# Splitting every product of the first down projection over the two 64-row halves of the array

## The chip, the cores and the metric

The kernel runs on one NeuronCore of a Trainium2 chip. The time of a kernel is that of one execution on the device, in microseconds (us). TensorE (PE in the rows) multiplies, VectorE (DVE) and ScalarE (ACT) work on tiles and take results out of PSUM, SyncE (SP) and GpSimd (POOL) issue transfers.

## The reference

One layer of a decoder trunk, 256 tokens of width 2048, in float32. Three attention branches and a gated merge come first; the change touches only the last step, the MLP:

```python
h = rms_norm(x, norm_mlp_pre[l])
u = jnp.square(jax.nn.relu(h @ w_up[l]))          # (256, 2048) @ (2048, 8192)
x = x + rms_norm(u @ w_down[l], norm_mlp_post[l]) # (256, 8192) @ (8192, 2048)
```

## The kernel before

**Numbers.** Each float32 operand is held as two float32r parts, a high and a low one. A product of two operands is three matmuls: high by high, high by low, low by high. ScalarE makes the high part of a weight tile (`w_hi`, L975), VectorE the low part (`w_lo`, L1367).

**Units.** Weights come in units: 256 rows of a weight matrix (two blocks k of 128) by 512 columns, 512 KB, in a ring of four slots. TensorE uses a unit in `unit` (L504 to L521): for each of the two token halves t, for each of the two k, three matmuls of 128 rows by 512 columns, 12 in all. The stationary operand is a 128 by 128 piece of the activations, which is loaded anew for each matmul (PEld, LDWEIGHTS); the moving operand is 512 columns of the weights. The results of token half t are summed in one PSUM bank.

**Chunks.** A chunk is all units of one set of 512 output columns. The first down projection, `down0`, has the first 4096 rows of `w_down`: 4 chunks of 16 units, the first written out, the other three a loop. So it has 4 x 16 x 12 = 768 matmuls. They use banks 0 (t = 0) and 1 (t = 1) in every chunk. `down1` does the same with the other 4096 rows and adds the result to that of `down0`, which waits in `y` in SBUF. Between them stands `up1`, which makes the second half of `u`; its first chunk uses banks 0 and 1 again. Transposes of `u` go through banks 6 and 7; in `down0` there is one group of 8, after the second unit of the first chunk.

**Emptying the banks.** The last matmul of token half 0 of a chunk raises `half_done`, the last of the chunk (as of each unit) raises `unit_used`. In `down0` before, VectorE copies bank 0 to `y` after `half_done` (`copy_out`, L1384) and raises `evac_v`, and ScalarE copies bank 1 after `unit_used` (L1336) and raises `evac_s`. In `down1` VectorE does both, by adding bank 0 or 1 to `y` (L1971). TensorE waits for these counts before the first matmul into a bank in the next chunk (`free`). In VectorE's order, which is the order of the code, the work on bank 0 stands ahead of the split of a weight unit that belongs to the last unit of the chunk, and (in `down1`) the work on bank 1 behind it. The splits run three units ahead (`LEAD`).

Of the kernel before, what the change touches and what calls it, by code (L numbers as in the profile page):

```python
# [21 lines left out]
ACT = mybir.ActivationFunctionType  # L22
AX = mybir.AxisListType.X

P = 128
# [5 lines left out]
W = 512  # L31
UR = 2
RING = 4
# [21 lines left out]
U0, C0 = {}, {}  # L55
# [5 lines left out]
UNITS = _u  # L61
UNITS_BEFORE_BRANCH = U0["branch"]

V_OF = {"gate": 0, "branch": 6, "out": 2, "down1": 2}
S_OF = {"branch": 0, "out": 2, "down1": 2, "gate": 2, "up0": 2, "up1": 2}
T_OF = {"v_a": 0, "v_c": 0, "gate": 0, "out": 0, "down0": 0, "down1": 0}
V0, S0, T0 = {}, {}, {}
_v = _s = _t = 0
# [93 lines left out]
def wait(eng, sem, value):  # L162

    if not (isinstance(value, int) and value <= 0):
        eng.wait_ge(sem, value)


def trunk(nc, x, rel_bias, w_in, cmp_k_pos, cmp_v_pos, cmp_k_w1, cmp_k_w2, cmp_v_w1, cmp_v_w2, diff_lambda,
# [10 lines left out]
    def sem(name):  # L179
        if name not in sems:  # L180
            sems[name] = ctx.enter_context(nc.semaphore(name))
        return sems[name]
# [53 lines left out]
    w_hi = put("ring", "w_hi", [P, RING, UR, W], F32R)  # L236
    w_lo = put("ring", "w_lo", [P, RING, UR, W], F32R)
# [24 lines left out]
    u_hi = put("u", "u_hi", [P, 32, SEQ], F32R, at=0)  # L262
    u_lo = put("u", "u_lo", [P, 32, SEQ], F32R, at=32768)
# [37 lines left out]
    y = put("f", "y", [P, 2, D], at=16384)  # L301
# [5 lines left out]
    ps = ctx.enter_context(nc.psum_tensor("ps", [P, 8, 512], F32))  # L307
# [195 lines left out]
    def _(pe):  # L503
# [19 lines left out]
        def chunk(u, n, hi, lo, kc, pair, cols=W, s0=0, between=(), free=None, before_last=None, ends=True):  # L523
            for j in range(n):
# [4 lines left out]
                if j == 1:  # L529
                    for f in between:  # L530
                        f()

        def half_pass(u, n, hi, lo, kc, t, first=0, before=None, free=()):

            for name, value in free:
                wait(pe, sem(name), value)
            tok = slice(t * P, (t + 1) * P)
            for j in range(first, n):
                if before and j in before:
                    before[j]()  # L540
                pe.wait_ge(sem("lo_ready"), (u + j).count(1))
                slot, c = (u + j).k % RING, kc + UR * j
                for k in range(UR):
                    a, b = j == 0 and k == 0, j == n - 1 and k == UR - 1
                    pe.matmul(ps[:, t, :], hi[:, c + k, tok], w_hi[:, slot, k, :], start=a, stop=False)
                    pe.matmul(ps[:, t, :], hi[:, c + k, tok], w_lo[:, slot, k, :], start=False, stop=False)
                    mm = pe.matmul(ps[:, t, :], lo[:, c + k, tok], w_hi[:, slot, k, :], start=False, stop=b)
                if t == 0 and j == n - 1:
                    mm.then_inc(sem("half_done"), 1)
                if t == 1:  # L550
                    mm.then_inc(sem("unit_used"), 1)
# [302 lines left out]
        for n in range(4):  # L854
            for b in range(3):
                before = sum(BR_UNITS[:b])
                t = Pos(T0["branch"] + n - 1)
                between = [] if (n == 0 or b != 1) else [
                    lambda t=t, n=n: transposed(t, lambda q, h: br_stage[:, (n - 1) % 2, h, q * P:(q + 1) * P],
                                                [("merge_done", n)])]  # L860
# [5 lines left out]
        def plain(name, i, n, hi, lo, between=(), before_last=None):  # L866

            if name.startswith("down") and isinstance(i, int):

                free = [[("evac_s", S0[name] - 3)], [("evac_s", S0[name] - 2)]]  # L870
            elif name == "out" and isinstance(i, int):

                free = [[("evac_v", V0[name] - 5)], [("evac_v", V0[name] - 4)]]
            elif name in ("out", "down1"):
                free = [[("evac_v", Pos(V0[name] + h, 2, i).count(-1))] for h in range(2)]
            else:
                free = [[("evac_v", Pos(V0[name], 1, i).count())], [("evac_s", Pos(S0[name], 1, i).count())]]
            chunk(Pos(U0[name], n, i), n, hi, lo, 0, 0, free=free, between=between, before_last=before_last)


# [2 lines left out]
            before_last=lambda: pe.wait_ge(sem("tevac_v"), T0["out"]))  # L883
# [52 lines left out]
        def up(name, i, between):  # L936

            for c in range(2):
                e = Pos(S0[name] + 2 * (c - 2), 4, i)
                free = [[("evac_s", e.count(1 + h))] for h in range(2)]  # L940
                if isinstance(i, int):

                    free = [[("evac_v", V0[name])], [("evac_s", S0[name])]] if c == 0 else None
                if name == "up0" and isinstance(i, int) and c == 0:
                    up_first()
                    continue
                chunk(Pos(U0[name] + CH * c, 2 * CH, i), CH, h_hi, h_lo, 0, c, free=free,
                      between=between if c == 0 else [up_tiles(name, 0, i)])
# [18 lines left out]
    def _(act):  # L967
# [234 lines left out]
        for n in range(NSLOT):  # L1202
            c, s = divmod(n, CH)
# [126 lines left out]
        def down(h, i):  # L1330
            u = Pos(U0[f"down{h}"], 16, i)
            chunk(u, 16, after={2: [lambda: t_split(Pos(T0[f"down{h}"] - 1), u_hi[:, 28:32, :])]} 
                  if isinstance(i, int) and i == 0 else None)
            if h == 0:
                act.wait_ge(sem("unit_used"), u.count(16))
                act.activation(y[:, 1, bass.ds(i * W, W)], ps[:, 1, :], ACT.Copy).then_inc(sem("evac_s"), 1)  # L1336
            else:
                product_squares("down1", 3, i)

        for h in range(2):  # L1340
# [18 lines left out]
    def _(dve):  # L1359
# [19 lines left out]
        def copy_out(dst, pair, half_done, scale=None):  # L1379

            dve.wait_ge(sem("half_done"), half_done)
            src = ps[:, 2 * pair, 0:dst.shape[-1]]
            if scale is None:
                dve.tensor_copy(dst, src).then_inc(sem("evac_v"), 1)  # L1384
            else:
                dve.tensor_scalar(dst, src, scale, None, ALU.mult).then_inc(sem("evac_v"), 1)
# [568 lines left out]
        def down(h, i):  # L1955
            u = Pos(U0[f"down{h}"], 16, i)
            after = {}
            if isinstance(i, int) and i == 0:
                after[2] = [lambda: t_split(Pos(T0[f"down{h}"] - 1), u_lo[:, 28:32, :], u_hi[:, 28:32, :])]
            elif h == 1:  # L1960
                after[3] = [lambda: gained(i - 1)]
            def evacuate(t):
                if h == 0:
                    copy_out(y[:, 0, bass.ds(i * W, W)], 0, Pos(C0["down0"], 1, i).count(1))
                    return
                if t == 0:
                    dve.wait_ge(sem("half_done"), Pos(C0["down1"], 1, i).count(1))
                else:
                    dve.wait_ge(sem("unit_used"), u.count(16))
                part = y[:, t, bass.ds(i * W, W)]  # L1970
                dve.tensor_tensor(part, ps[:, t, :], part, ALU.add).then_inc(sem("evac_v"), 1)  # L1971

            chunk(u, 16, after=after, early=lambda: evacuate(0))
            if h == 1:
                evacuate(1)

        for h in range(2):
            up(f"up{h}", 0)
# [85 lines left out]
```

## Time and profile before

| | us |
|---|---|
| time, median of 3 runs | 1747.69 |
| lowest and highest of them | 1746.37, 1749.54 |
| the profiled execution's own time | 1748.23 |
| its span, first to last instruction | 1746.9 |
| TensorE busy | 1716.4 |
| VectorE busy | 950.1 |
| ScalarE busy | 839.5 |

An engine's busy time is the union of its instructions. Matmuls are pipelined: one of 512 columns is shown as 0.39 us, while the next starts 0.23 us after it. So the time between starts is what counts on TensorE, and busy time only tells that it never ran dry.

### The profile page before, as it was taken

To read this page: it belongs to the slowest core of one execution; us is meant where nothing else is said; L and a number is where in the kernel's file an instruction comes from. 1 tells how busy PE (TensorE), PEld (TensorE's weight loads), DVE (VectorE), ACT (ScalarE), POOL (GpSimd) and SP (SyncE) were. 2 spreads that over 40 slices of the span, in tenths; PEclk is the share of its full clock that TensorE was granted. 3 is DMA by queue.
4 is the path that set the end of the run, shared out by engine and by line. 5 is a ranking of instruction groups with operands and counts; after the bars stand their busy time and mean duration, and the time that the engine had idled before them with its cause. 6 is when DMAs were issued, how large, how long until landed. Compare 5 with 4: busy or idle time off the path is not lost.

```text
span 1746.9 us, 23954 instructions
## 1 busy us (share of the span) xinstructions
PE 1716.4 (98%) x8155; PEld 1400.9 (80%) x8155; DVE 950.1 (54%) x1338; ACT 839.5 (48%) x1269; POOL 55.2 (3%) x103
## 2 busy tenths in 40 slices
PE   7999999999999999999999989999999999999997
PEld 6888877877777888788888768888888888888886
DVE  5544465755555554455765575555444455554455
ACT  5444456655655554434444464444433344444442
POOL 1000010000000002000000000000000000000000
PEclk9999999999999999999999999999999999999999
DMA  7666665655566768657766556665555666655654
GB/s 235 200 189 182 193 187 133 178 163 162 172 170 174 221 199 264 215 176 246 272 228 232 189 171 180 184 188 182 193 194 193 191 189 184 191 183 189 192 191 137
DMA packets 168278, 336.77 MB, mean 193 GB/s; under 512 B 11408, under 2 KB 13664, under 8 KB 167680
## 3 DMA queue, kind: packets, MB, share of 16 engines
q1 hardware_dynamic: 162512, 317.17, 59.0%
q0 software_dynamic: 5552, 18.44, 4.3%
q8 instruction: 51, 0.84, 0.2%
q14 instruction: 35, 0.29, 0.0%
q10 hardware_dynamic: 128, 0.03, 0.0%
HBM read 327.11 MB, written 8.49 MB: 192 GB/s over the span
## 4 chain that ended last, share of the span: by engine, by line
PE 93%; DVE 3%; ACT 2%; DMA 1%; issue 1%; SPq 0%; DVEq 0%; ACTq 0%
PE ps L516 20%; PE ps L518 20%; PE ps L517 20%; PE ps L665 9%; PE ps L666 8%; PE ps L667 8%; PE ps L562 1%; DMA raw<-in_w_in_dram 1%; PE ps L745 1%; PE ps L723 1%; DVE w_lo L1367 1%; PE ps L708 1%; PE ps L705 1%; ACT w_hi L975 1%; ACT logits L1128 1%
## 5 line engine op out<-in xcount | busy, mean ns | idle before, releaser
L1367 DVE TENSOR_TENSOR w_lo<-raw,w_hi 128x1024 fp32r<-128x1024 f32 x576 | 702.7, 1225 | 672.2 <-ACT w_hi L975 654.3
L975 ACT ACTIVATE w_hi<-raw 128x1024 fp32r<-128x1024 f32 x576 | 605.6, 1057 | 627.9 <-PE ps L518 537.6
L516 PE MATMUL ps<-w_hi,h_hi 128*128 128x512 f32 x896 | 353.2, 394 | 3.3 <-DVE h_lo L1439 1.6
L518 PE MATMUL ps<-w_hi,h_lo 128*128 128x512 f32 x896 | 349.9, 391 | 0.0
L517 PE MATMUL ps<-w_lo,h_hi 128*128 128x512 f32 x896 | 349.6, 390 | 0.0
L665 PE MATMUL ps<-w_hi,h_hi 128*128 128x512 f32 (+1 forms) x704 | 279.5, 397 | 2.6 <-DVE w_lo L1367 2.5
L666 PE MATMUL ps<-w_lo,h_hi 128*128 128x512 f32 (+1 forms) x704 | 273.1, 388 | 0.0
L667 PE MATMUL ps<-w_hi,h_lo 128*128 128x512 f32 (+1 forms) x704 | 272.8, 388 | 0.0
L516 PEld LDWEIGHTS ps<-w_hi,h_hi 128*128 128x128 f32 x896 | 168.7, 188 | 40.8 <-DVE h_lo L1439 2.0
L518 PEld LDWEIGHTS ps<-w_hi,h_lo 128*128 128x128 f32 x896 | 168.7, 188 | 35.6
L517 PEld LDWEIGHTS ps<-w_lo,h_hi 128*128 128x128 f32 x896 | 168.9, 188 | 34.2
L516 PE MATMUL ps<-w_hi,u_hi 128*128 128x512 f32 x496 | 193.4, 390 | 0.0
L517 PE MATMUL ps<-w_lo,u_hi 128*128 128x512 f32 x496 | 193.0, 389 | 0.0
L518 PE MATMUL ps<-w_hi,u_lo 128*128 128x512 f32 x496 | 193.0, 389 | 0.0
L665 PEld LDWEIGHTS ps<-w_hi,h_hi 128*128 128x128 f32 x704 | 132.8, 189 | 42.6 <-issue 12.5
L667 PEld LDWEIGHTS ps<-w_hi,h_lo 128*128 128x128 f32 x704 | 133.0, 189 | 27.4
L666 PEld LDWEIGHTS ps<-w_lo,h_hi 128*128 128x128 f32 x704 | 133.0, 189 | 24.7
L516 PEld LDWEIGHTS ps<-w_hi,u_hi 128*128 128x128 f32 x496 | 93.1, 188 | 20.1 <-DVE y L1971 0.9
L518 PEld LDWEIGHTS ps<-w_hi,u_lo 128*128 128x128 f32 x496 | 93.1, 188 | 19.4
L517 PEld LDWEIGHTS ps<-w_lo,u_hi 128*128 128x128 f32 x496 | 93.1, 188 | 19.0
L1128 ACT ACTIVATE logits<-logits,negmax 128x128 f32<-128x128 f32 x96 | 42.6, 444 | 48.2 <-DVE negmax L1583 48.2
L516 PE MATMUL ps<-w_hi,o_hi 128*128 128x512 f32 x160 | 62.6, 391 | 0.8 <-issue 0.8
(276 smaller groups left out, 1167.3 us busy)
## 6 DMA issues: line engine op xcount, KB each, us to landing
raw<-in_w_in_dram SPq DMA_DIRECT2D x240, 512.0 KB, 3.6
raw<-in_w_up_dram SPq DMA_DIRECT2D x128, 512.0 KB, 3.8
raw<-in_w_down_dram SPq DMA_DIRECT2D x128, 512.0 KB, 3.8
raw<-in_w_out_dram SPq DMA_DIRECT2D x32, 512.0 KB, 4.5
bias<-bias_table POOLq DMA_DIRECT2D x72, 128.0 KB, 3.7
raw<-in_w_branch_b_dram SPq DMA_DIRECT2D x16, 512.0 KB, 5.8
raw<-in_w_branch_c_dram SPq DMA_DIRECT2D x16, 512.0 KB, 5.2
gate_dram<-stage SPq DMA_DIRECT2D x12, 512.0 KB, 6.1
```

Source lines behind the costliest of these rows:

```text
L516: pe.matmul(acc, hi[:, kc + k, tok], w_hi[:, slot, k, 0:cols], start=a, stop=False)
L517: pe.matmul(acc, hi[:, kc + k, tok], w_lo[:, slot, k, 0:cols], start=False, stop=False)
L518: mm = pe.matmul(acc, lo[:, kc + k, tok], w_hi[:, slot, k, 0:cols], start=False, stop=b)
L562: tr = pe.transpose(ps[:, T_BANK + q // 2, 256 * (q % 2) + P * h:256 * (q % 2) + P * h + P], source(q, h), ident[:, :])
L665: pe.matmul(acc, h_hi[:, kc, tok], w_hi[:, slot, k, 0:cols], start=kc == 0, stop=False)
L666: pe.matmul(acc, h_hi[:, kc, tok], w_lo[:, slot, k, 0:cols], start=False, stop=False)
L667: mm = pe.matmul(acc, h_lo[:, kc, tok], w_hi[:, slot, k, 0:cols], start=False, stop=kc == KC - 1)
L705: pe.matmul(ps[:, 2 + d, 0:P], q[half[d], pr.q_tile, 0:P], k[half[d], pr.k_tile, 0:P], start=True, stop=True)
L708: pe.matmul(ps[:, 2 + d, P:3 * P], q[half[d], pr.q_tile, P:2 * P], k[half[d], pr.k_tile, :], start=True, stop=True).then_inc(sem("scores_r ...
L975: act.activation(w_hi[:, slot, :, :], raw[:, slot, :, :], ACT.Copy).then_inc(sem("hi_ready"), 1)
L1128: e = act.activation(part, part, ACT.Exp, bias=top, scale=-1.0, accum_out=total)
L1367: dve.tensor_tensor(w_lo[:, slot, :, :], raw[:, slot, :, :], w_hi[:, slot, :, :].bitcast(F32), ALU.subtract).then_inc(sem("lo_ready"), 1)
```

## The change

A new function, `row_unit`, takes the place of `unit` in `down0`. It splits each 128-row matmul into two of 64 rows: r = 0 has partitions 0 to 63 of both operands and sums into bank t, r = 1 has partitions 64 to 127 and sums into bank 4 + t. Each is still 512 columns wide, and each loads its own stationary operand of 64 by 128. At the end of a chunk two banks hold a token half. VectorE copies bank 4 + t to `y`, waits for its own copy, and adds bank t to it; ScalarE's copy is gone. TensorE's next chunk (and `up1` behind the last) waits for VectorE's additions, for token half 0 and 1 apart.

```diff
-V_OF = {"gate": 0, "branch": 6, "out": 2, "down1": 2}
-S_OF = {"branch": 0, "out": 2, "down1": 2, "gate": 2, "up0": 2, "up1": 2}
+V_OF = {"gate": 0, "branch": 6, "out": 2, "down0": 2, "down1": 2}
+S_OF = {"branch": 0, "out": 2, "down0": 0, "down1": 2, "gate": 2, "up0": 2, "up1": 2}
...
+        def row_unit(u, slot, kc, first=False, last=False, free=None):
+            pe.wait_ge(sem("lo_ready"), u.count(1))
+            for t in range(2):
+                if free is not None:
+                    for name, value in free[t]:
+                        wait(pe, sem(name), value)
+                tok = slice(t * P, (t + 1) * P)
+                for k in range(UR):
+                    a, b = first and k == 0, last and k == UR - 1
+                    for r in range(2):
+                        rows = slice(64 * r, 64 * r + 64)
+                        pe.matmul(ps[:, 4 * r + t, :], u_hi[rows, kc + k, tok], w_hi[rows, slot, k, :], start=a, stop=False)
+                    for r in range(2):
+                        rows = slice(64 * r, 64 * r + 64)
+                        pe.matmul(ps[:, 4 * r + t, :], u_hi[rows, kc + k, tok], w_lo[rows, slot, k, :], start=False,
+                                  stop=False)
+                    for r in range(2):
+                        rows = slice(64 * r, 64 * r + 64)
+                        mm = pe.matmul(ps[:, 4 * r + t, :], u_lo[rows, kc + k, tok], w_hi[rows, slot, k, :], start=False,
+                                       stop=b)
+                if last and t == 0:
+                    mm.then_inc(sem("half_done"), 1)
+            mm.then_inc(sem("unit_used"), 1)
...
-            elif name in ("out", "down1"):
+            else:
                 free = [[("evac_v", Pos(V0[name] + h, 2, i).count(-1))] for h in range(2)]
-            else:
-                free = [[("evac_v", Pos(V0[name], 1, i).count())], [("evac_s", Pos(S0[name], 1, i).count())]]
+            if name == "down0":
+                for j in range(n):
+                    if before_last and j == n - 2:
+                        before_last()
+                    row_unit(Pos(U0[name], n, i) + j, j % RING, UR * j, j == 0, j == n - 1, free if j == 0 else None)
+                    if j == 1:
+                        for f in between:
+                            f()
+                return
...
-                    free = [[("evac_v", V0[name])], [("evac_s", S0[name])]] if c == 0 else None
+                    free = [[("evac_v", V0[name] - 1 + t)] for t in range(2)] if c == 0 else None
...
-            if h == 0:
-                act.wait_ge(sem("unit_used"), u.count(16))
-                act.activation(y[:, 1, bass.ds(i * W, W)], ps[:, 1, :], ACT.Copy).then_inc(sem("evac_s"), 1)
-            else:
+            if h == 1:
                 product_squares("down1", 3, i)
...
             def evacuate(t):
-                if h == 0:
-                    copy_out(y[:, 0, bass.ds(i * W, W)], 0, Pos(C0["down0"], 1, i).count(1))
-                    return
                 if t == 0:
-                    dve.wait_ge(sem("half_done"), Pos(C0["down1"], 1, i).count(1))
+                    dve.wait_ge(sem("half_done"), Pos(C0[f"down{h}"], 1, i).count(1))
                 else:
                     dve.wait_ge(sem("unit_used"), u.count(16))
                 part = y[:, t, bass.ds(i * W, W)]
+                if h == 0:
+                    dve.tensor_copy(part, ps[:, 4 + t, :]).then_inc(sem("high_copied"), 1)
+                    dve.wait_ge(sem("high_copied"), Pos(t + 1, 2, i).count())
+                    dve.tensor_tensor(part, ps[:, t, :], part, ALU.add).then_inc(sem("evac_v"), 1)
+                    return
                 dve.tensor_tensor(part, ps[:, t, :], part, ALU.add).then_inc(sem("evac_v"), 1)
 
             chunk(u, 16, after=after, early=lambda: evacuate(0))
-            if h == 1:
-                evacuate(1)
+            evacuate(1)
```

How this stands on the engines. On TensorE, the start of one unit of the looped chunks of `down0`, before (L516 to L518 are the three matmuls of `unit`):

```order
L516 MATMUL ps<-w_hi,u_hi 128x512 [waits lo_ready]
L517 MATMUL ps<-w_lo,u_hi 128x512
L518 MATMUL ps<-w_hi,u_lo 128x512
L516 MATMUL ps<-w_hi,u_hi 128x512
L517 MATMUL ps<-w_lo,u_hi 128x512
```

and the same place of the changed kernel:

```order
L546 MATMUL ps<-w_hi,u_hi 128x512 [waits lo_ready]
L546 MATMUL ps<-w_hi,u_hi 128x512
L549 MATMUL ps<-w_lo,u_hi 128x512 x2
L553 MATMUL ps<-w_hi,u_lo 128x512 x2
L546 MATMUL ps<-w_hi,u_hi 128x512 x2
```

Each matmul has become two of the same width (r = 0 and r = 1), next to each other; a unit has 24 instead of 12, and nothing else moved on TensorE.

On VectorE, the end of a looped chunk of `down0`, before (L1367 is the split of a weight unit, L1384 the copy of bank 0):

```order
L1367 TENSOR_TENSOR w_lo<-raw,w_hi 128x1024 [waits unit_used,hi_ready]
L1381 REGISTER_ALU
L1384 ISA [waits half_done]
L1384 COPY y<-ps 128x512
L1364 REGISTER_ALU
L1367 TENSOR_TENSOR w_lo<-raw,w_hi 128x1024 [waits unit_used,hi_ready]
L1984 REGISTER_ALU
L1984 COMPARE_AND_BRANCH
```

and in the changed kernel (L1398 is the split, L2001 the copy of bank 4 + t, L2003 the addition of bank t):

```order
L1398 TENSOR_TENSOR w_lo<-raw,w_hi 128x1024 [waits unit_used,hi_ready]
L1995 REGISTER_ALU
L2001 ISA [waits half_done]
L2001 COPY y<-ps 128x512
L2002 ISA
L2003 TENSOR_TENSOR y<-ps,y 128x512 [waits high_copied]
L1395 REGISTER_ALU
L1398 TENSOR_TENSOR w_lo<-raw,w_hi 128x1024 [waits unit_used,hi_ready]
L2001 ISA [waits unit_used]
L2001 COPY y<-ps 128x512
L2002 REGISTER_ALU
L2003 TENSOR_TENSOR y<-ps,y 128x512 [waits high_copied]
```

One copy ahead of the split has become a copy and an addition, and behind the split there now stand another copy and addition, for token half 1.

## Rows read from the trace of the kernel before

**Rows 1.** The page: span, busy time by engine, granted TensorE clock in tenths.

```profile
span 1746.9 us, 23954 instructions
...
PE 1716.4 (98%) x8155; PEld 1400.9 (80%) x8155; DVE 950.1 (54%) x1338; ACT 839.5 (48%) x1269; POOL 55.2 (3%) x103
...
PEclk9999999999999999999999999999999999999999
```

**Rows 2.** The page: the chain that ended last, by engine.

```profile
PE 93%; DVE 3%; ACT 2%; DMA 1%; issue 1%; SPq 0%; DVEq 0%; ACTq 0%
```

**Rows 3.** Busy time in a window over `down0`: sum, each engine, clock, DMA share, GB/s.

```profile
1207.09:1381.60 174.51, 174.51 (x775) 144.59 (x774) 81.89 (x69) 70.84 (x69) 0.00 (x0) 1.00 0.59 192
```

**Rows 4.** Instructions of L1336: count, ns (least/median/most), first and last start.

```profile
L1336 ACT ACTIVATE y<-ps x4: 598/599/600, 1251.7 to 1382.4; 128x512 f32 x3, 128x512 f32<-128x512 f32 x1
```

**Rows 5.** Timeline, end of the first chunk of `down0`: start, length, instruction.

```profile
1250.34 0.69 DVE L1384 COPY y<-ps 128x512 f32<-128x512 f32 x1 [1.70 <-PE ps L518]
...
1251.27 0.39 PE L518 MATMUL ps<-w_hi,u_lo 128*128 128x512 f32 x1
...
1251.50 0.39 PE L516 MATMUL ps<-w_hi,u_hi 128*128 128x512 f32 x1
```

**Rows 6.** Timeline, end of the first chunk of `down1`.

```profile
1605.35 0.39 PE L518 MATMUL ps<-w_hi,u_lo 128*128 128x512 f32 x1
...
1605.58 0.39 PE L516 MATMUL ps<-w_hi,u_hi 128*128 128x512 f32 x1
...
1605.78 0.69 DVE L1971 TENSOR_TENSOR y<-ps,y 128x512 f32<-128x512 f32 x1 [1.70 <-PE ps L518]
...
1606.38 1.22 DVE L1367 TENSOR_TENSOR w_lo<-raw,w_hi 128x1024 fp32r<-128x1024 f32 x1
...
1606.94 0.39 PE L516 MATMUL ps<-w_hi,u_hi 128*128 128x512 f32 x1
...
1607.52 0.69 DVE L1971 TENSOR_TENSOR y<-ps,y 128x512 f32<-128x512 f32 x1
...
1608.07 0.39 PE L518 MATMUL ps<-w_hi,u_lo 128*128 128x512 f32 x1
...
1608.26 0.19 PEld L516 LDWEIGHTS ps<-w_hi,u_hi 128*128 128x128 f32 x1 [0.22 <-DVE y L1971]
1608.30 0.46 PE L516 MATMUL ps<-w_hi,u_hi 128*128 128x512 f32 x1
...
1608.60 0.39 PE L517 MATMUL ps<-w_lo,u_hi 128*128 128x512 f32 x1
```

**Rows 7.** Timeline, two VectorE instructions of which the second waits for the first.

```profile
1010.80 0.16 DVE L1854 TENSOR_REDUCE ssq<-ssq_parts 128x1 f32<-128x4 f32 x1 [3.85 <-ACT squares L1007]
1010.99 0.15 DVE L1855 TENSOR_SCALAR mean<-ssq 128x1 f32<-128x1 f32 x1
```

**Rows 8.** Groups by shape: 64-row pairs (L708), 128-row (L810); union busy us, mean ns.

```profile
L708 PE MATMUL ps<-k_b,q_b 64*128 64x256 f32 x64 | 9.6, 377 | 0.0
L810 PE MATMUL ps<-cmp_pt,vc_diag 128*128 128x256 f32 x16 | 3.6, 379 | 0.0
```

**Rows 9.** The same view, the stationary loads of L708.

```profile
L708 PEld LDWEIGHTS ps<-k_b,q_b 64*128 64x128 f32 x64 | 4.9, 188 | 0.0
```

**Rows 10.** Timeline, 128-row matmuls, then 32 in 32-column strips (L760), then 128-row ones.

```profile
731.07 0.39 PE L667 MATMUL ps<-w_hi,h_lo 128*128 128x512 f32 x1
731.38 1.93 PE L760 MATMUL ps<-w1v,blocks_t 128*32 128x256 f32 x32
733.25 0.50 PE L665 MATMUL ps<-w_hi,h_hi 128*128 128x512 f32 x1
733.59 0.40 PE L666 MATMUL ps<-w_lo,h_hi 128*128 128x512 f32 x1
```

**Rows 11.** Instructions of L661 in one window: a wait in TensorE's sequencer.

```profile
L661 PEldq EVENT_SEMAPHORE  x1: 51/51/51, 731.9 to 731.9; - x1
```

**Rows 12.** Instructions of L655 in one window: its next wait, 12 matmuls later.

```profile
L655 PEldq EVENT_SEMAPHORE  x1: 51/51/51, 732.5 to 732.5; - x1
```

## The prediction

> **What bounds the kernel now.** I read the page first. TensorE is busy for 1716.4 of 1746.9 us at a clock that stays at the higher level (2.4 GHz, every tenth 9) [rows 1], and the chain that ended last lies on it for 93% [rows 2]. The window over `down0` says the same of this stage: TensorE busy for all of 174.51 us, clock 1.00, VectorE 81.89, ScalarE 70.84, the transfers at 0.59 of their engines [rows 3]. So only what changes the spacing of matmuls, or makes TensorE wait, moves the time. The other engines have half their time free, on average; whether they are free at the right moment has to be read at the ends of chunks.
>
> The spacing comes from ScalarE's copies, one for each chunk's end: four of them start from 1251.7 to 1382.4, so a chunk takes 130.7 / 3 = 43.57 us [rows 4], and its 192 matmuls start 0.2269 us apart. At the end of a chunk nothing is lost: the next chunk's first matmul starts 0.23 us after the last one of the old, with VectorE's copy of bank 0 long done [rows 5].
>
> **The change, term by term.**
>
> *The products.* 768 matmuls become 1536 of the same width. If the halves of the array work one after the other, the stage doubles; if they work side by side, each pair takes the place of one matmul. The trace has 64-row pairs, in the attention scores. One score at L708 is four records of 377 ns (two matmuls in float32, each in two passes of 256 columns). 16 scores have a union of 9.6 us, 0.600 each [rows 8]; less one record, 0.223 us lie between the first start and the last. One after the other it would be three spacings. The nearest 128-row group, L810, has 16 records in 3.6 us, a spacing of (3.6 - 0.379) / 15 = 0.215 [rows 8]. So a score has one spacing, 0.215, and a lag of 0.007 for the second of a pair: the pair runs side by side at the price of one. Their stationary loads overlap too: four of 188 ns have a union of 4.9 / 16 = 0.306 us a score [rows 9].
>
> There is one gap in this evidence. A float32 pass needs 0.215 us for 256 columns, a float32r matmul 0.2269 for 512, so the pairs here must take columns and write sums twice as fast as those of the scores. I see no row against it, and take the pair at the price of one 128-row matmul: 0 us. The bounds are those of the rivals below.
>
> *The sequencer.* It must now issue four records (two loads, two matmuls) in 0.227 us. Around the strips of L760 it catches up, and its waits show how fast: the wait of L661 at 731.9 and that of L655 at 732.5 have 12 matmuls with their loads between them [rows 11, 12], 0.05 us for a matmul with its load. Two need 0.10 of 0.227 us: no cost.
>
> *Changes between whole array and halves.* Going from 128-row matmuls to strips took 731.38 - 731.07 = 0.31 us instead of 0.23. Going back, the last strip started at 731.38 + 1.93 - 0.38 = 732.93, the next matmul at 733.25 (0.32 instead of 0.22) and its follower 0.34 later instead of 0.23 [rows 10]: about 0.2 us. `down0` has four such changes (in, out and in around the transposes of the first chunk, out). At 0.2 each that is 0.8 us; 0.4 to 1.6 are possible.
>
> *The ends of the chunks.* This is the largest term. I lay VectorE's new order over the times of `down1`, where VectorE already does both banks [rows 6]. Let T be its start at 1605.78, after the last matmul of token half 0 (1605.35). TensorE then does token half 1 from 1605.58 and would start the next chunk at 1606.94, T + 1.16.
> - Copy of bank 4: 0.69 us, as an addition or copy of this size takes [rows 5, 6]. The addition waits for it; between dependent instructions VectorE needs 0.03 us (1010.80 + 0.16 to 1010.99) [rows 7]. The addition starts at T + 0.72 and ends at T + 1.41.
> - TensorE's load follows the end of an addition by 0.05 us and its matmul that by 0.04 (1607.52 + 0.69 = 1608.21, 1608.26, 1608.30), and the matmul behind it comes 0.30 instead of 0.23 later [rows 6]. So the next chunk starts at T + 1.50: 0.34 late, with 0.07 behind it.
> - The split starts 0.60 after the addition (1605.78 to 1606.38), at T + 1.32, and keeps VectorE for 1.14 (1606.38 to 1607.52) [rows 6]. The copy of bank 5 starts at T + 2.46; its wait, `unit_used`, is long met. Copy and addition end at T + 3.87, and the first matmul of token half 1 can start at T + 3.96.
> - TensorE wants it after the six products of token half 0, at 1.16 + 0.41 + 6 x 0.2269 = T + 2.93. It waits 1.03 us, and loses 0.07 more.
>
> That is 0.41 + 1.10 = 1.5 us an end, and there are four: three inside `down0`, and one ahead of `up1`, which waits for the same additions. Nothing absorbs it, since TensorE sets the end: 6.0 us. The bounds: with 0.60 instead of 0.72 from copy to addition, as between instructions that don't wait for each other [rows 6], an end costs 1.27 and the four 5.1; with 0.2 us for the refill of the loads behind each wait, as after a change in [rows 10], instead of 0.07, an end costs 1.77 and the four 7.1. Behind the two additions on VectorE stands only the next split, which is three units (8 us) ahead of its use. ScalarE loses four copies of 0.6 us [rows 4], which were hidden, so nothing comes back.
>
> The Trainium skill, "TensorEngine Tiling (Array Packing)", section PSUM Bottleneck, says the same as a warning: tiling speeds TensorE up and not the emptying of PSUM, and both ScalarE and VectorE should be used for it. The change goes against it by giving all four banks to VectorE.
>
> *Sum.* 0 + 0 + 0.8 + 6.0 = 6.8 us. The profiled execution took 1748.23, so 1755.0 by it; it is 0.54 above the median of the runs, 1747.69, and against that I say **1754.5 us**, 0.4% slower.
>
> **Rivals.**
>
> *A. The split hides the gap between matmuls: no slower.* The 128-row float32 group has 0.215 us between starts, the float32r products 0.2269 [rows 4, 8], and the clock is at its upper level throughout [rows 1]. If these 0.011 us are a changeover of one array half that the other half fills, 768 pairs gain 8.8 us (0.0115 each). TensorE then wants the banks a little sooner, so the ends cost 6.5 instead of 6.0: 1747.7 - 8.8 + 0.8 + 6.5 = 1746.2. A gain of 0.009 us a pair is the point at which the change pays for itself. For it: the scores' pairs show 0.215, not 0.227. Against it: they are float32, and so is the 128-row group with 0.215; splitting took nothing off there. Each half has still to change its own operand for each product. Chance 0.18.
>
> The Trainium skill, "TensorE: Matmul & The Clock Gate", section Back-to-back issue gap, gives N / 2.4 + 2.5 ns for warm matmuls, some 216 ns at 512 columns, as if the gap were not there at all; the trace has 0.2269, so the measurement decides, and by the page's figure the products of this stage would take some 8 us less.
>
> *B. The float32r halves do not run side by side.* Wholly in turn: 768 x 0.2269 = 174 us more, the waits at the ends nearly gone since a token half then takes 2.7 us: about 1923. Or only the loads are exposed, 0.11 us a pair by the follower in [rows 10]: 768 x 0.11 = 84, about 1839. For it: no float32r pair is in the trace, and these need twice the rate. Against it: the overlap of the scores is complete, in other banks, on the same rows. Chance 0.12.
>
> *C. The lag of 0.007 us is paid by every pair.* 768 x 0.007 = 5.4 us more: 1759.9. For it: nothing but that the lag exists; against it: the spacing of like records within the scores is not longer. Chance 0.10.
>
> **How the numbers follow.** The forecast has 0.60 (its own range 1752 to 1757.5, from ends at 5.1 to 7.1 us, changes at 0.4 to 1.6 and a unit of spread), A 0.18, C 0.10, B 0.12. The range leaves out B and takes in A and C with 1 to 2 us of spread: 1745 to 1762. A measurement of this kernel can tell a change of 0.2%, 3.5 us, from none. Slower by more than that are B, C and nearly all of the forecast; A lies within it, and with ends at their lower bound and the runs' own spread below the median it comes to 1744: faster 0.06, same 0.19, slower 0.75.
>
> **What would show it.** In the profile of the changed kernel: L546, L549 and L553 with 1536 records, starting in pairs some 0.007 us apart with 0.227 between pairs (0.216 would be A, 0.45 B, 0.234 C); a span of `down0` near 181 us; TensorE idle ahead of L546 (and of L516 in `up1`) on VectorE's L2003, 0.3 us for token half 0 and 1.0 for token half 1, four times each. The prediction would be wrong if the pairs' spacing is not 0.227, or if VectorE's two additions come earlier than T + 1.41 and T + 3.87.

## The result, and the profile after

| | before | changed |
|---|---|---|
| time, median of 6 runs, us | 1747.84 | 1754.61 |
| lowest and highest | 1746.37, 1749.88 | 1752.57, 1758.53 |
| the profiled execution's own time | 1748.23 | 1756.29 |
| span | 1746.9 | 1755.0 |

The changed kernel takes 1.0045 of the time before (95% interval 1.0032 to 1.0059), 6.8 us more by the medians. 1754.5 was forecast.

The page of the changed kernel: span, busy times, granted clock, and the group of the first product of each pair (busy us, mean ns, idle before it and what ended it).

```profile
span 1755.0 us, 25501 instructions
...
PE 1720.7 (98%) x8923; PEld 1401.1 (80%) x8923; DVE 957.6 (55%) x1350; ACT 837.3 (48%) x1265; POOL 55.0 (3%) x103
...
PEclk9999999999999999999999999999999999999999
...
L546 PE MATMUL ps<-w_hi,u_hi 64*128 64x512 f32 x512 | 100.6, 390 | 3.1 <-DVE y L2003 3.1
```

Against [rows 1]: TensorE has 768 matmuls more (8923 to 8155) and is busy for 4.3 us more, where 768 matmuls in turn would be 174. The clock is the same. The new idle time on it is put down to L2003, VectorE's addition.

The end of the second chunk of `down0` in the timeline of the changed kernel, the place of [rows 5]:

```profile
1297.03 0.69 DVE L2001 COPY y<-ps 128x512 f32 x1 [1.88 <-PE ps L553]
...
1297.76 0.69 DVE L2003 TENSOR_TENSOR y<-ps,y 128x512 f32 x1
1297.84 0.39 PE L553 MATMUL ps<-w_hi,u_lo 64*128 64x512 f32 x2
...
1298.37 1.22 DVE L1398 TENSOR_TENSOR w_lo<-raw,w_hi 128x1024 fp32r<-128x1024 f32 x1
1298.50 0.51 PE L546 MATMUL ps<-w_hi,u_hi 64*128 64x512 f32 x2 [0.27 <-DVE y L2003]
1298.84 0.40 PE L549 MATMUL ps<-w_lo,u_hi 64*128 64x512 f32 x2
...
1299.50 0.68 DVE L2001 COPY y<-ps 128x512 f32 x1
...
1299.79 0.39 PE L553 MATMUL ps<-w_hi,u_lo 64*128 64x512 f32 x2
...
1300.22 0.69 DVE L2003 TENSOR_TENSOR y<-ps,y 128x512 f32 x1
...
1300.96 0.49 PE L546 MATMUL ps<-w_hi,u_hi 64*128 64x512 f32 x2 [0.79 <-DVE y L2003]
1301.30 0.39 PE L549 MATMUL ps<-w_lo,u_hi 64*128 64x512 f32 x2
```

Here the reader sees the forecast chain. Each "x2" of 0.39 us is a pair, whose second starts at most 0.01 us behind the first. The last pair of the old chunk starts at 1297.84, the first of the new one at 1298.50, 0.66 later instead of 0.23, when the first addition (1297.76 + 0.69) is done. The next follows 0.34 later instead of 0.23. Then token half 1: from 1299.79 to 1300.96 are 1.17 us instead of 0.23, and the second addition ends at 1300.91.

For the length of the stage, the first matmul of `down0` and the first of `up1` are taken. In the kernel before:

```profile
1207.09 0.39 PE L516 MATMUL ps<-w_hi,u_hi 128*128 128x512 f32 x1
...
1382.06 0.39 PE L516 MATMUL ps<-w_hi,h_hi 128*128 128x512 f32 x1
```

and in the changed one, with the wait for token half 1 in `up1`, which lies behind that point:

```profile
1208.06 0.50 PE L546 MATMUL ps<-w_hi,u_hi 64*128 64x512 f32 x2
...
1388.96 0.47 PE L516 MATMUL ps<-w_hi,h_hi 128*128 128x512 f32 x1 [0.35 <-DVE y L2003]
...
1391.33 0.50 PE L516 MATMUL ps<-w_hi,h_hi 128*128 128x512 f32 x1 [0.76 <-DVE y L2003]
```

174.97 and 180.90 us: 5.9 more. The wait in `up1` is worth 1.1 (from its first matmul to the first of `down1` it is 181.6 us instead of 180.5). Together 7.0 us. The stages ahead of `down0` end 1.0 us later in this execution, though the two programs issue the same work there: over the runs below, `down0` starts anywhere from 1203.7 to 1209.2. It goes with the granted clock ahead of the stage: from 600 to 850 us of the span that is 0.98 in this execution, 0.99 in that of the kernel before, and 1.00 in the one that starts `down0` at 1203.7. This is why stage lengths say more than whole times here.

### The profile page after: what moved, and what is told of

Same layout as the page of the kernel before. It is cut to its first block, busy times and chain, and to the rows that moved or that the text cites. A ratio compares the mean times of both kernels' runs of the same rounds, so it can differ in the third digit from the quotient of the medians.

```text
span 1755.0 us, 25501 instructions
## 1 busy us (share of the span) xinstructions
PE 1720.7 (98%) x8923; PEld 1401.1 (80%) x8923; DVE 957.6 (55%) x1350; ACT 837.3 (48%) x1265; POOL 55.0 (3%) x103
## 4 chain that ended last, share of the span: by engine, by line
PE 93%; DVE 3%; ACT 2%; DMA 1%; issue 1%; SPq 0%; DVEq 0%; ACTq 0%
PE ps L516 17%; PE ps L518 17%; PE ps L517 17%; PE ps L691 9%; PE ps L692 8%; PE ps L693 8%; PE ps L546 3%; PE ps L553 3%; PE ps L549 3%; PE ps L588 1%; PE ps L771 1%; PE ps L749 1%; DMA raw<-in_w_in_dram 1%; DVE w_lo L1398 1%; PE ps L734 1%
## 5 line engine op out<-in xcount | busy, mean ns | idle before, releaser
L1398 DVE TENSOR_TENSOR w_lo<-raw,w_hi 128x1024 fp32r<-128x1024 f32 x576 | 702.5, 1224 | 672.4 <-ACT w_hi L1009 651.4
L516 PE MATMUL ps<-w_hi,h_hi 128*128 128x512 f32 x896 | 353.1, 394 | 4.4 <-DVE h_lo L1470 1.6
L518 PE MATMUL ps<-w_hi,h_lo 128*128 128x512 f32 x896 | 349.8, 390 | 0.0
L516 PEld LDWEIGHTS ps<-w_hi,h_hi 128*128 128x128 f32 x896 | 168.8, 188 | 42.8 <-issue 2.5
L518 PEld LDWEIGHTS ps<-w_hi,h_lo 128*128 128x128 f32 x896 | 168.6, 188 | 35.5
L546 PE MATMUL ps<-w_hi,u_hi 64*128 64x512 f32 x512 | 100.6, 390 | 3.1 <-DVE y L2003 3.1
L549 PE MATMUL ps<-w_lo,u_hi 64*128 64x512 f32 x512 | 99.8, 386 | 0.0
L553 PE MATMUL ps<-w_hi,u_lo 64*128 64x512 f32 x512 | 99.7, 386 | 0.0
L516 PE MATMUL ps<-w_hi,u_hi 128*128 128x512 f32 x240 | 93.8, 391 | 0.0
L518 PE MATMUL ps<-w_hi,u_lo 128*128 128x512 f32 x240 | 93.4, 389 | 0.0
L517 PE MATMUL ps<-w_lo,u_hi 128*128 128x512 f32 x240 | 93.4, 389 | 0.0
L516 PE MATMUL ps<-w_hi,o_hi 128*128 128x512 f32 x160 | 62.6, 391 | 0.8 <-issue 0.8
```

Of the source, the lines that this page charges most:

```text
L516: pe.matmul(acc, hi[:, kc + k, tok], w_hi[:, slot, k, 0:cols], start=a, stop=False)
L517: pe.matmul(acc, hi[:, kc + k, tok], w_lo[:, slot, k, 0:cols], start=False, stop=False)
L518: mm = pe.matmul(acc, lo[:, kc + k, tok], w_hi[:, slot, k, 0:cols], start=False, stop=b)
L546: pe.matmul(ps[:, 4 * r + t, :], u_hi[rows, kc + k, tok], w_hi[rows, slot, k, :], start=a, stop=False)
L549: pe.matmul(ps[:, 4 * r + t, :], u_hi[rows, kc + k, tok], w_lo[rows, slot, k, :], start=False, stop=False)
L553: mm = pe.matmul(ps[:, 4 * r + t, :], u_lo[rows, kc + k, tok], w_hi[rows, slot, k, :], start=False, stop=b)
```

## The experiments

Each kernel was timed beside the kernel before on the same chip. "The stage" is the length of `down0` as above; a loss in `up1` is named beside it. The cuts of code show the lines that matter and shorten others.

**Whole matmuls, two banks.** The ends of the chunks as changed, the products as before:

```diff
-                    for r in range(2):
-                        rows = slice(64 * r, 64 * r + 64)
-                        pe.matmul(ps[:, 4 * r + t, :], u_hi[rows, kc + k, tok], w_hi[rows, slot, k, :], start=a, stop=False)
+                    acc = ps[:, 4 * k + t, :]
+                    pe.matmul(acc, u_hi[:, kc + k, tok], w_hi[:, slot, k, :], start=first, stop=False)
```

(and so for the other two products).

> The matmuls of down0 are whole again (128 rows, 768 of them), but the two 128-row blocks k of a unit sum into different banks (k = 0 into bank t, k = 1 into bank 4 + t), so that the ends of the chunks are those of the changed kernel, copy and addition on VectorE. If the ends of the chunks are the cost (my theory): four ends at about 1.5 us, and nothing for changes between whole array and halves, 1747.8 + 6.0 = 1754, within 1 us of the changed kernel. If the cost lies in the 64-row products or in the changes of array shape: about 1748.

Measured: 1753.16 us, ratio 1.0038 (1.0024 to 1.0051). The timeline of this kernel:

```profile
1204.46 0.39 PE L544 MATMUL ps<-w_hi,u_hi 128*128 128x512 f32 x1
...
1384.83 0.47 PE L516 MATMUL ps<-w_hi,h_hi 128*128 128x512 f32 x1 [0.35 <-DVE y L1995]
```

The stage is 180.37 us, and `up1` loses 1.2: 6.6 us over before, without one 64-row product. The ends of the chunks are the cost, for the most part.

**Each product split, no wait at the ends.** Every other chunk sums into other banks. For that the loop over the chunks 1 to 3 is written out on TensorE and VectorE, which the cut does not show:

```diff
-                        pe.matmul(ps[:, 4 * r + t, :], u_hi[rows, kc + k, tok], w_hi[rows, slot, k, :], start=a, stop=False)
+                        pe.matmul(ps[:, base + 4 * r + t, :], u_hi[rows, kc + k, tok], w_hi[rows, slot, k, :], start=a, stop=False)
...
+                             2 * (i % 2))
```

> The changed kernel with every product split over the halves, but chunks 0 and 2 of down0 sum into banks 0, 1, 4, 5 and chunks 1 and 3 into 2, 3, 6, 7 (the loop over chunks 1 to 3 written out on TensorE and VectorE), so that no chunk waits for the emptying of the one ahead. By my theory pairs cost what a whole matmul costs and only the four changes of array shape are left, 0.8 us: 1747.8 + 0.8 = 1748.6. If the split products themselves cost time: 1754 or so. If the 0.003 us by which pairs start closer in the changed kernel's trace than whole matmuls were a gain: 1748 at best.

Measured: 1747.26 us, ratio 1.0006 (0.9995 to 1.0017). The timeline of this kernel:

```profile
1206.70 0.50 PE L546 MATMUL ps<-w_hi,u_hi 64*128 64x512 f32 x2
...
1382.27 0.50 PE L516 MATMUL ps<-w_hi,h_hi 128*128 128x512 f32 x1
```

175.57 us, 0.6 more than before, and at most 0.1 lost in `up1` (180.6 us against 180.5 to the first matmul of `down1`). TensorE is busy without a gap. So 768 pairs of float32r matmuls, with twice the column rate of the pairs in [rows 8], cost what 768 whole ones cost, and what is left for the four changes of shape is 0.6 together. Since the run with whole matmuls has the ends without the changes (6.6) and this one the changes without the ends (0.6), they add to 7.2, and the changed kernel has 7.0. This is also the best version of the split among these runs, and it doesn't beat the kernel before.

**The split of a weight unit last.**

```diff
+            if h == 0:
+                chunk(u, 16, after=after, early=lambda: [evacuate(0), evacuate(1)])
+                return
             chunk(u, 16, after=after, early=lambda: evacuate(0))
             evacuate(1)
```

> The changed kernel, with one thing moved: at the end of each chunk of down0 VectorE does copy and addition of token half 1 ahead of the split of a weight unit instead of behind it. If that split holds up bank 1 (my theory), the wait of about 1.05 us a chunk end before token half 1 goes, since copy and addition then end some 2.9 us after VectorE's start, when TensorE wants the bank; 0.4 to 0.5 us for token half 0 stay: 1754.6 - 4 x 1.05 = 1750.4. If the wait is set by something else than VectorE's order, or the late split makes a new wait: 1754 or more.

Measured: 1749.63 us, ratio 1.0011 (1.0002 to 1.0020). The timeline of this kernel:

```profile
1203.66 0.50 PE L546 MATMUL ps<-w_hi,u_hi 64*128 64x512 f32 x2
...
1381.33 0.47 PE L516 MATMUL ps<-w_hi,h_hi 128*128 128x512 f32 x1 [0.35 <-DVE y L2003]
```

177.67 us, and at most 0.1 lost in `up1`: 2.7 over before, where the changed kernel has 7.0. Moving one instruction of 1.2 us behind two others took 4.3 us off, 1.1 for each of four ends, and the later split made no new wait. The wait for token half 1 was set by VectorE's order.

**ScalarE makes the copies, VectorE only adds.**

```diff
+            if h == 0:
+                for t in range(2):
...
+                    act.activation(y[:, t, bass.ds(i * W, W)], ps[:, 4 + t, :], ACT.Copy).then_inc(sem("high_copied"), 1)
-                    dve.tensor_copy(part, ps[:, 4 + t, :]).then_inc(sem("high_copied"), 1)
```

with the split last, as above.

> The changed kernel, but ScalarE copies bank 4 + t to y (0.60 us) and VectorE only adds bank t, both token halves ahead of VectorE's split. By my theory token half 0 is free 0.60 + 0.04 + 0.69 us after the start, 1.42 with the release, against 1.16 wanted: 0.26 late and 0.10 for the refill; token half 1 is not waited for. Four times 0.36, with 0.8 for the changes of shape: 1747.8 + 2.2 = 1750.0, 0.4 us less than with VectorE alone and the split last. If the two readers get in each other's way, or the dependency between engines costs more than VectorE's own: 1751 or more.

Measured: 1749.89 us, ratio 1.0016 (1.0007 to 1.0025), what the run with VectorE alone gave, not 0.4 less. The timeline of this kernel, at the end of a looped chunk, shows why:

```profile
1291.62 0.60 ACT L1374 ACTIVATE y<-ps 128x512 f32 x1 [0.39 <-PE ps L553]
...
1292.37 0.69 DVE L2009 TENSOR_TENSOR y<-ps,y 128x512 f32 x1 [2.60 <-ACT y L1374]
...
1293.11 0.50 PE L546 MATMUL ps<-w_hi,u_hi 64*128 64x512 f32 x2 [0.27 <-DVE y L2009]
```

The copy is 0.09 us shorter than VectorE's, but the addition follows its end by 0.15 us (1292.22 to 1292.37) and not by the 0.04 between VectorE's own (1297.72 to 1297.76, in the changed kernel). The shorter copy is lost in the handover. My expectation took for it the 0.04 of VectorE's own instructions, and that was too little even in the chunk that is written out, where it is 0.10 (1248.14 to 1248.24). The two engines work here one after the other on each token half; a division of the banks between them was not run.

**The halves in another order.** Three products of rows 0 to 63, then three of rows 64 to 127:

```diff
                 for k in range(UR):
-                    for r in range(2):
-                        pe.matmul(... u_hi, w_hi)
-                    for r in range(2):
-                        pe.matmul(... u_hi, w_lo)
-                    for r in range(2):
-                        mm = pe.matmul(... u_lo, w_hi)
+                    for r in range(2):
+                        pe.matmul(... u_hi, w_hi)
+                        pe.matmul(... u_hi, w_lo)
+                        mm = pe.matmul(... u_lo, w_hi)
```

> The changed kernel with another order within a block k: first the three products of rows 0 to 63, then the three of rows 64 to 127, instead of pair by pair. If the array starts matmuls in program order and two run together only when they are neighbours on different halves (my theory), six matmuls take four spacings instead of three: 256 spacings of 0.2267 us more, 1754.6 + 58 = 1813, and the longer token half covers some of the waits at the ends (0 to 6 us less). If TensorE looked ahead and filled the idle half: 1755. If each waited for the one before it: 1754.6 + 174 = 1928.

Measured: 1754.70 us, ratio 1.0049 (1.0034 to 1.0065), as the changed kernel. My theory's 1813 fell; 1755 stood beside it for a TensorE that looks ahead. The timeline of this kernel at the first matmuls of `down0`, where TensorE has just come from whole matmuls (L547, L548, L549 are the three products, in both halves):

```profile
1209.23 0.50 PE L547 MATMUL ps<-w_hi,u_hi 64*128 64x512 f32 x2
1209.57 0.40 PE L548 MATMUL ps<-w_lo,u_hi 64*128 64x512 f32 x2
1209.80 0.40 PE L549 MATMUL ps<-w_hi,u_lo 64*128 64x512 f32 x2
1210.03 0.40 PE L547 MATMUL ps<-w_hi,u_hi 64*128 64x512 f32 x2
```

In the program three matmuls of one half stand ahead of the first of the other. Yet two L547 lie within 0.50 us, ahead of both L548, and the pairs are 0.23 us apart as in the changed kernel: the other half's first matmul started before two that precede it in the program.

**Twelve and twelve.** The same with all products of a unit: `for r` outside `for t` and `for k`. At a chunk's start TensorE now waits for both token halves' banks before its first matmul.

> The changed kernel, with the products of a unit in yet another order: first all twelve of rows 0 to 63 (both token halves), then all twelve of rows 64 to 127. With three and three the array's second half ran 0.010 us behind the first, so TensorE had started matmuls ahead of others in the program. If each half of the array takes its own next matmul from the queue, and 24 records (12 loads, 12 matmuls) fit into it: pairs 12 x 0.0033 = 0.04 us apart, 0.227 between pairs, 1754 to 1757. If it looks less far ahead: the halves run partly in turn, up to 174 us more.

Measured: 1993.64 us, ratio 1.1411 (1.1388 to 1.1434). The timeline of this kernel in the first chunk (L548, L549, L550 are the products; granted clock 1.00):

```profile
1230.15 0.39 PE L550 MATMUL ps<-w_hi,u_lo 64*128 64x512 f32 x1
1230.16 0.60 PE L548 MATMUL ps<-w_hi,u_hi 64*128 64x512 f32 x2
1230.49 0.50 PE L549 MATMUL ps<-w_lo,u_hi 64*128 64x512 f32 x2
1230.72 0.49 PE L550 MATMUL ps<-w_hi,u_lo 64*128 64x512 f32 x2
1230.95 0.39 PE L548 MATMUL ps<-w_hi,u_hi 64*128 64x512 f32 x1
...
1231.88 0.39 PE L549 MATMUL ps<-w_lo,u_hi 64*128 64x512 f32 x1
1232.11 0.39 PE L550 MATMUL ps<-w_hi,u_lo 64*128 64x512 f32 x1
1232.12 0.62 PE L548 MATMUL ps<-w_hi,u_hi 64*128 64x512 f32 x2
```

The halves run side by side only at the turn from one to the other. At 1230.15 the ninth matmul of one half starts, and 0.01 us later the first of the other, ahead of three that precede it in the program. The rows marked x2 hold the last three of the one and the first three of the other. Then five run alone (1230.95 to 1231.88), until the next turn at 1232.11. Twelve take 1.96 us (1230.16 to 1232.12) instead of 1.36. So in these two runs TensorE finds work for the idle half up to three matmuls (with their loads) further on, and no more. Over the 128 times twelve matmuls of the stage that would be 77 us, and the ends of the chunks add to it: at the first of them TensorE waits 2.8 us (1271.93 to 1274.91 instead of 0.23). The windows over this kernel's first chunk and the rest of `down0` (clock, the third number from the end) show where the remainder of the 246 us went:

```profile
1207.00:1270.00 63.00, 63.00 (x383) 53.58 (x382) 20.66 (x17) 18.22 (x18) 0.00 (x0) 1.00 0.39 134
1276.00:1627.00 351.00, 347.76 (x1149) 288.03 (x1148) 63.16 (x57) 49.68 (x47) 0.00 (x0) 0.50 0.21 71
```

From shortly after the first chunk's end the granted clock was 0.50 (1.2 GHz).

**One half only.** The products of rows 64 to 127 are left out in `down0` (`for r in range(1)`), so half of the sum is missing.

> The changed kernel without the products of rows 64 to 127 in down0 (so half of that sum is left out, and the copies still read banks 4 and 5). 768 matmuls of 64 rows are left. By my theory a matmul of 64 rows costs what one of 128 rows costs, and the second of a pair costs nothing: 1754.6, with 0.227 us between starts. If a pair had a price of its own, or a 64-row matmul alone were quicker than one of 128 rows (0.216 us between starts, the spacing of the float32 group), the stage would be up to 8 us shorter: 1747.

Measured: 1866.61 us, ratio 1.0691 (1.066 to 1.0722), which none of my theories had. The timeline of this kernel around the end of the first chunk, and two windows of it:

```profile
1253.69 0.39 PE L553 MATMUL ps<-w_hi,u_lo 64*128 64x512 f32 x1
1254.23 0.50 PE L546 MATMUL ps<-w_hi,u_hi 64*128 64x512 f32 x1 [0.15 <-DVE y L2003]
...
1255.49 0.39 PE L553 MATMUL ps<-w_hi,u_lo 64*128 64x512 f32 x1
1256.69 0.50 PE L546 MATMUL ps<-w_hi,u_hi 64*128 64x512 f32 x1 [0.81 <-DVE y L2003]
1257.02 0.43 PE L549 MATMUL ps<-w_lo,u_hi 64*128 64x512 f32 x1
1257.26 0.62 PE L553 MATMUL ps<-w_hi,u_lo 64*128 64x512 f32 x1
1257.69 0.62 PE L546 MATMUL ps<-w_hi,u_hi 64*128 64x512 f32 x1
```

```profile
1209.00:1250.00 41.00, 41.00 (x184) 33.05 (x184) 19.60 (x17) 17.39 (x17) 0.00 (x0) 1.00 0.53 182
1257.30:1499.50 242.20, 242.20 (x569) 185.94 (x567) 64.08 (x58) 49.63 (x47) 0.00 (x0) 0.50 0.31 103
```

In the first chunk it was as expected: 0.227 us between starts, so a 64-row matmul alone costs what a pair or a whole one costs. After the waits of 0.3 us (1253.69 to 1254.23 instead of 0.23) and 1.0 us (1255.49 to 1256.69) at the chunk's end the granted clock fell from 2.4 to 1.2 GHz, and each start came 0.43 us after the last to the end of the stage.

**One half only, without the waits.** The same cut in the kernel with banks of its own for each chunk; half of the sum is missing here too.

> Only the products of rows 0 to 63 are left in down0 (so half of that sum is left out), as in the run before with one half, but the chunks sum into banks of their own, so that TensorE waits at no chunk's end. There the granted clock fell to 1.2 GHz after the waits at the end of the first chunk, and stayed there to the end of down0 (0.427 us between starts instead of 0.227). If the waits had a part in the fall: the clock stays at 2.4 GHz, 1748. If half an empty array alone lets it fall, sooner or later in the stage: 0.427 us from some point on, up to 1747 + 768 x 0.2 = 1900.

Measured: 1748.12 us, ratio 1.0009 (0.9998 to 1.0019). The window over its `down0`:

```profile
1206.30:1381.90 175.60, 175.60 (x777) 142.02 (x777) 88.13 (x79) 69.30 (x66) 0.00 (x0) 1.00 0.58 192
```

The clock stayed at its upper level. Half the array idle did not let it fall here, and the waits alone did not in the changed kernel, which has the same ones; in the run with both it fell.

**384 columns.** The kernel before, with `cols=384` in `down0`; the last 128 columns of each chunk's sums are left out.

> The kernel before, with matmuls of 384 instead of 512 columns in down0 (the last 128 columns of each chunk's sums are left out). Tells what the 0.0134 us between the 0.2133 us that 512 columns need at 2.4 GHz and the 0.2267 us between starts is. If a fixed price of each matmul: 0.1600 + 0.0134 = 0.1734 us between starts, 768 x 0.0533 = 41 us less than before, 1707. If it grows with the columns (the moving operand comes 6% too slowly): 0.1700 us, 1704. If a float32r matmul with a new stationary operand can't be quicker than the load allows: more than 0.174.

Measured: 1706.29 us, ratio 0.9773 (0.9744 to 0.9801), two runs. The timeline of this kernel:

```profile
1240.04 0.33 PE L516 MATMUL ps<-w_hi,u_hi 128*128 128x384 f32 x1
...
1241.08 0.33 PE L516 MATMUL ps<-w_hi,u_hi 128*128 128x384 f32 x1
```

Six starts in 1.04 us, 0.1733 each: 0.1600 at 2.4 GHz and 0.0133, as with 512 columns. So it is a price of each float32r matmul, not a slower flow of columns. It is not quite the same at every width: in the attention branches of the kernel before, float32r matmuls of 304 columns start 0.1377 us apart (30 of them from 306.72 to 310.85), 0.0110 above the 0.1267 that the same reckoning gives.

**A change of shape with each unit.** In the kernel with banks of their own, every second unit is multiplied whole, 64 changes instead of 4:

```diff
+                    if j % 2:
+                        unit(Pos(U0[name], n, i) + j, j % RING, hi, lo, UR * j, i % 2, W, False, j == n - 1)
+                    else:
+                        row_unit(Pos(U0[name], n, i) + j, j % RING, UR * j, j == 0, j == n - 2, free if j == 0 else None,
+                                 2 * (i % 2))
```

> The kernel with banks of their own for the chunks (down0 0.6 us longer than before, with 4 changes of array shape), in which every second unit is multiplied whole instead of in halves: 64 changes of shape in place of 4. If a change costs 0.15 us, as that 0.6 over four of them says: 60 x 0.15 = 9 us more, 1756.5. By the 0.2 us that I took before the result: 12 us, 1759. If a change inside a running stream of products is cheaper than one at a wait or around transposes: less than 1752.

Measured: 1762.78 us, ratio 1.0082 (1.0066 to 1.0099), more than any of the three. The timeline of this kernel at two changes:

```profile
1232.02 0.39 PE L518 MATMUL ps<-w_hi,u_lo 128*128 128x512 f32 x1
1232.34 0.50 PE L546 MATMUL ps<-w_hi,u_hi 64*128 64x512 f32 x2
1232.68 0.40 PE L549 MATMUL ps<-w_lo,u_hi 64*128 64x512 f32 x2
...
1234.99 0.39 PE L553 MATMUL ps<-w_hi,u_lo 64*128 64x512 f32 x2
1235.31 0.50 PE L516 MATMUL ps<-w_hi,u_hi 128*128 128x512 f32 x1
```

0.32 instead of 0.23 at the change, 0.34 instead of 0.23 behind it, and then some ten spacings that are a little longer: from 1232.34 to 1235.31, twelve matmuls take 2.97 us, 0.25 more than 12 x 0.2267. Back again it is the same, 2.97 us from 1235.31 to 1238.28. 60 x 0.25 = 15 us is what it cost (1762.78 to 1747.26).

## Why the prediction was right

The forecast was 6.8 us by the sum 0 + 0 + 0.8 + 6.0; the traces have 7.0, as 0 + 0 + 0.6 + 6.4.

*The products.* At no cost, as taken from the scores. The open point, whether float32r pairs run side by side at twice the column rate, is settled by the kernel with banks of their own. Rival B falls with that.

*The sequencer.* It issued 24 matmuls and 24 loads a unit with no gap, at 2.72 us a unit (12 x 0.2267).

*Changes of shape.* 0.6 us against 0.8: right by two errors against each other, so partly luck. The price of one in a running stream is 0.25, above my 0.2. But two of the four stand at the transposes, where the stream is broken anyway: from the last matmul ahead of them to the second behind them it is 1.33 us in the kernel before (1212.30 to 1213.63) and 1.68 in the one with banks of its own (1212.07 to 1213.75), 0.35 more for two changes.

*The ends of the chunks.* The forecast laid VectorE's start at T and had the additions end at T + 1.41 and T + 3.87. In the looped end shown above, T is 1297.03 and they end at T + 1.42 and T + 3.88. What was off is T itself: in the loop VectorE starts 0.12 us later than in a chunk that is written out, 0.55 behind the start of the last matmul of token half 0 (1296.48) and not 0.43. The likely cause is that each copy in the loop has a register instruction of 57 to 65 ns just ahead of it (six in the trace, the first at 1296.9), and those that are written out have none; no run isolates it. Three of the four ends are in the loop, and I had laid all four over a written-out one. So token half 0 was wanted at T + 1.04 and not T + 1.16, and waited 0.43 us instead of 0.34, and token half 1 0.94 instead of 1.03; the refill behind each wait was 0.11 instead of 0.07. An end costs 1.6 us instead of 1.5. My upper bound of 1.77 for an end was wrongly added: a slower refill behind token half 0 takes as much off the wait for token half 1, so 0.2 us for each refill makes 1.64 an end and 6.6 for the four, not 7.1. The measured 6.4 lies within either.

*Rival A,* that splitting hides the 0.0115 us between the two spacings of [rows 4, 8] (0.2269 and 0.215 differ by 0.012, which makes 9 us and not 8.8): it does not. The stage with pairs and no waits is 0.6 us longer than before and not 8.8 shorter, and the 384-column run shows these 0.013 us to be a price of each float32r matmul; each half pays it for its own. The Trainium skill, "TensorE: Matmul & The Clock Gate", section Back-to-back issue gap, would have 2.5 ns in this place by its formula for the gap of a single matmul; the runs have 13, so the measurement decides. *Rival C* falls too: the second of a pair starts within 0.01 us of the first and pairs stay 0.227 apart.

The warning in the Trainium skill, "TensorEngine Tiling (Array Packing)", section PSUM Bottleneck, is of a faster TensorE whose PSUM is emptied no faster. Here TensorE is not faster, but it fills twice the banks, and the trace agrees in so far as all that the split cost came from the emptying of PSUM but 0.6 us. Its advice to use both engines for it, taken as a copy on ScalarE ahead of each addition on VectorE, gained nothing at this size (1749.89 us against 1749.63), where the order on VectorE gained 4.3 us.

## What to carry to other kernels

In these runs, splitting a full 128-row product over two halves of the array buys nothing: the halves run side by side, so they cost one matmul, but a whole matmul already cost that. What it adds is a second accumulator, and its price is read at the chunk's end from VectorE's order, not from busy shares: put the work that frees a bank ahead of work that is needed later, or give the next chunk other banks. Where halves are used for small contractions, keep products of different halves within three matmuls of each other in the program: three and three cost nothing here, twelve and twelve did, and nothing between was run.

## What the runs showed of the hardware that I had not expected

- TensorE starts matmuls out of program order across array halves: with three of one half ahead of three of the other, both halves ran together (1754.70 us); with twelve and twelve (1993.64 us) they overlapped only at the turns, and a half's first matmul started ahead of three that precede it. The Trainium skill, "TensorE: Matmul & The Clock Gate", Part 3, section The mechanism, has matmuls in strict order of the program; these traces differ from it, and they decide.
- With half of the array idle and waits at a chunk's end, the granted clock fell from 1.00 to 0.50 for the rest of the stage (1866.61 us, and 1993.64 with twelve and twelve, where the halves mostly take turns). With half of the array idle and no waits it stayed at 1.00 (1748.12 us), and with both halves in use and waits it did too (1754.61 us). What in the two together lets it fall is open.
- A change between whole array and halves costs 0.25 us in a running stream of products (1762.78 us with 60 more of them), of which 0.20 lie in the first two spacings.
